# Latent attention with three-pass scores, joint keys of two heads, and the query factor inside the exponential

## The reference, cut to what matters

```python
def queries(cq, rotate):
    q = (_rms(cq) * q_norm) @ w_uq                              # 512 -> 16 heads x 96
    q = _rms(q.reshape(*q.shape[:2], MLA_HEADS, MLA_QK)) * q_gain
    return _rope_tail(q, cos, sin) if rotate else q             # rotates the last 32 of 96

def keys_values(ckv, k_rope, rotate):
    ukv = ((_rms(ckv) * kv_norm) @ w_ukv).reshape(..., MLA_HEADS, MLA_NOPE + MLA_V)
    k_nope, v = ukv[..., :MLA_NOPE], ukv[..., MLA_NOPE:]        # 64 and 64
    k_rope = jnp.broadcast_to(k_rope[:, :, None, :], ...)       # one rope part for all heads
    k = _rms(jnp.concatenate([k_nope, k_rope], axis=-1)) * k_gain
    return (_rope_tail(k, cos, sin) if rotate else k), v

s = jnp.einsum('bqhd,bkhd->bhqk', qi, k).astype(jnp.float32) * 96 ** -0.5
p = jax.nn.softmax(s, axis=-1)
out = jnp.einsum('bhqk,bkhd->bqhd', p, v)
```

## Time and profile before

| | us |
|---|---|
| median of three runs | 3789.0 |
| profiled execution, its own time | 3790.6 |
| its span, first to last instruction | 3787.6 |
| PE busy in the span | 3653.7 (96%) |
| DVE, ACT, POOL busy | 1750.0, 1493.2, 1263.2 |
| chain that ended last | PE 62%, DVE 5%, ACT 2%, issue 1% |
| mean granted TensorE clock | 0.987 of full speed |

### The profile page before, as it was taken

One profiled execution on the slowest core, in us unless ns is written; L12 is line 12 of the kernel. 1 busy time (PEld: TensorE's weight loads), 2 busy tenths in 40 slices (PEclk: granted clock), 3 DMA queues, 4 the chain that ended last, 5 costly groups with the idle time before them and its releaser, 6 DMA issues.

```text
span 3787.6 us, 53426 instructions
## 1 busy us (share of the span) xinstructions
PE 3653.7 (96%) x19878; PEld 2903.4 (77%) x19878; DVE 1750.0 (46%) x2574; ACT 1493.2 (39%) x2501; POOL 1263.2 (33%) x524
## 2 busy tenths in 40 slices
PE   7999999999989999999999999899989999999998
PEld 5875788888866667888777778688867777877886
DVE  4766652333456665443555552511156555252114
ACT  4343431222355553332555552422235555333222
POOL 3530422232320112444423334344433333434443
PEclk9999999999989999999999999999999999999999
DMA  5367212111210002322212213232222222222222
GB/s 210 115 226 293 82 63 67 61 62 64 75 61 17 23 23 73 100 97 97 95 62 68 68 68 100 69 104 94 95 78 73 68 68 68 89 84 84 99 94 89
DMA packets 84706, 333.79 MB, mean 88 GB/s; under 512 B 9520, under 2 KB 9648, under 8 KB 78000
## 3 DMA queue, kind: packets, MB, share of 16 engines
q1 hardware_dynamic: 83808, 329.22, 25.4%
q10 hardware_dynamic: 720, 2.10, 0.2%
HBM read 329.18 MB, written 2.10 MB: 87 GB/s over the span
## 4 chain that ended last, share of the span: by engine, by line
PE 62%; DVE 5%; ACT 2%; issue 1%; DVEq 0%; ACTq 0%
PE pB L2263 13%; PE pB L274 12%; PE pB L275 12%; PE pB L276 12%; PE pT L2321 1%; PE pT L1756 1%; DVE arena L901 1%; PE pO L2348 1%; PE pS L2293 1%; PE pB L1730 1%; PE pS L1747 1%; PE pO L274 1%; PE pO L276 1%; PE pO L275 1%; PE pO L2343 1%
## 5 line engine op out<-in xcount | busy, mean ns | idle before, releaser
L2828 POOL TENSOR_TENSOR w_lo<-w_raw,w_hi 128x1024 fp32r<-128x1024 f32 x520 | 1263.0, 2430 | 2502.3 <-ACT w_hi L320 2501.7
L274 PE MATMUL pB<-h_hi,w_hi 128*128 128x512 f32 x2102 | 832.2, 396 | 38.7 <-DVE h_lo L2756 15.5
L275 PE MATMUL pB<-h_lo,w_hi 128*128 128x512 f32 x2102 | 823.9, 392 | 0.0
L276 PE MATMUL pB<-h_hi,w_lo 128*128 128x512 f32 x2102 | 823.5, 392 | 0.0
L320 ACT ACTIVATE w_hi<-w_raw 128x1024 fp32r<-128x1024 f32 x520 | 547.6, 1053 | 479.7 <-PE pB L276 315.0
L274 PEld LDWEIGHTS pB<-h_hi,w_hi 128*128 128x128 f32 x2102 | 399.5, 190 | 134.1 <-issue 40.1
L276 PEld LDWEIGHTS pB<-h_hi,w_lo 128*128 128x128 f32 x2102 | 399.0, 190 | 83.8
L275 PEld LDWEIGHTS pB<-h_lo,w_hi 128*128 128x128 f32 x2102 | 399.9, 190 | 81.9 <-issue 1.2
L274 PE MATMUL pB<-b_hi,w_hi 128*128 128x512 f32 (+1 forms) x1080 | 399.6, 370 | 7.6 <-POOL w_lo L2828 6.5
L275 PE MATMUL pB<-b_lo,w_hi 128*128 128x512 f32 (+1 forms) x1080 | 394.7, 365 | 0.0
L276 PE MATMUL pB<-b_hi,w_lo 128*128 128x512 f32 (+1 forms) x1080 | 394.6, 365 | 0.0
(11 more groups left out here) (527 smaller groups left out, 5140.5 us busy)
## 6 DMA issues: line engine op xcount, KB each, us to landing
w_raw<-stream SPq DMA_DIRECT2D x520, 512.0 KB, 3.3
under<-ada SPq DMA_DIRECT2D x42, 1024.0 KB, 4.8
arena<-ada SPq DMA_DIRECT2D x6, 1024.0 KB, 17.2
x<-xT SPq DMA_DIRECT2D x1, 2048.0 KB, 8.2
out<-x SPq DMA_DIRECT2D x8, 256.0 KB, 2.1
...
```

Of the source, the lines that this page charges most:

```text
L274: pe.matmul(dst, lh, rh, start=(begin and k == 0), stop=False)
L275: pe.matmul(dst, lh, rl, start=False, stop=False)
L276: last = pe.matmul(dst, ll, rh, start=False, stop=(end and k == len(pairs) - 1))
L2828: pool.tensor_tensor(w_lo[:, s, :], w_raw[:, s, :], w_hi[:, s, :].bitcast(F32), ALU.subtract).then_inc(lo_ready, 1)
```

## The change

Four things change in the latent attention, and nothing outside it:
- Scores are three fp32r passes over split halves `mla_q` and `mla_k` (buffers by head parity, high in 0 and 1, low in 2 and 3) in place of one f32 product of `qf` and `kf`.
- K and C project the 64 plain key features of two heads at once, one on partitions 0 to 63, the other on 64 to 127; the odd head of a pair has its rope rows below its plain ones. The rope part of the key is multiplied by the factor on POOL (`pool_key_rope`).
- Squares of the rope rows are summed once ahead (turn SR), scaled and added on POOL to the squares of the keys (`pool_key_squares`), and one product with a matrix of two blocks of ones gives the sums of both heads.
- Query sums become eight products with one column, and the query factor, one number per query, is the `scale` of the exponential.

```diff
         def turns_beside(p):
-            a, b, g = 2 * p + 2, 2 * p + 3, p // 2
-            if p + 1 == PAIRS_A:
+            q, g = p + 1, p // 2
+            if q == PAIRS_A:
                 return [[] for _ in range(8)]
-            if p % 2:
-                return [[("K", a)], [("C", p + 1)], [("SQ", a), ("SK", a)], [("SC", p + 1), ("Q", b)], [("K", b)], [("SQ", b)],
-                        [("SK", b)], []]
-            return [[("K", a)], [("C", p + 1), ("K", b)], [("V", 3 * g), ("V", 3 * g + 1)], [("SQ", a), ("SK", a)],
-                    [("V", 3 * g + 2), ("SC", p + 1)], [("Q", b)], [("SQ", b), ("SK", b)], []]
+            values = [("V", 3 * g + i) for i in range(3)] if p % 2 == 0 else []
+            return [[("K", q)], [("C", q)] + values[0:1], [("Q", 2 * q + 1)], [("SK", q), ("SC", q)], values[1:2] + [("SQ", q)],
+                    values[2:3], [], []]
...
-        FIRST_TURNS = [("Q", 0), ("Q", 1), ("K", 0), ("K", 1), ("SQ", 0), ("SK", 0), ("C", 0), ("SC", 0), ("SQ", 1), ("SK", 1)]
+        FIRST_TURNS = [("Q", 0), ("Q", 1), ("SR", 1), ("SR", 0), ("SQ", 0), ("K", 0), ("C", 0), ("SK", 0), ("SC", 0)]
...
             elif what == "SQ":
-                pe.wait_ge(q_sq, n + 1)
-                pe.matmul(dst[0:QK_A, :], o96, hsq_q[n % 2][0:QK_A, :], start=True, stop=True).then_inc(q_sum, 1)
+                pe.wait_ge(q_sq, 2 * n + 2)
+                for e in range(2):
+                    rows_of = (const("upto")[:, QK_A - 1:QK_A], const("from")[:, ROPE:ROPE + 1])[e]
+                    for t in range(TB):
+                        last = pe.matmul(dst[:, e * TB + t:e * TB + t + 1], hsq_q[e][:, t * P:(t + 1) * P], rows_of, start=True, stop=True)
+                last.then_inc(q_sum, 1)
             elif what == "SK":
-                pe.wait_ge(k_sq, n + 1)
-                pe.matmul(dst[0:QK_A, :], o96, hsq_l[n % 2][0:QK_A, :], start=True, stop=True).then_inc(k_sum, 1)
+                pe.wait_ge(kr_step, 4)
+                pe.wait_ge(k_total, 2 * n + 1)
+                pe.matmul(dst, by_pair, hsq_k[1], start=True, stop=True).then_inc(k_sum, 1)
...
-            lhs = qf[0:QK_A, n % 4, t * P:(t + 1) * P]
-            pe.matmul(score[u % 2][:, 0:512], lhs, kf[0:QK_A, n % 4, 0:512], start=True, stop=True)
-            pe.matmul(score[u % 2][:, 512:TC], lhs, kf[0:QK_A, n % 4, 512:TC], start=True, stop=True).then_inc(a_s, 1)
+            pe.wait_ge(q_low, n + 1)
+            e = n % 2
+            r, o = ROWS_A[e], slice(t * P, (t + 1) * P)
+            q_hi, q_lo, k_hi, k_lo = mla_q[r, e, o], mla_q[r, 2 + e, o], mla_k[r, e, :], mla_k[r, 2 + e, :]
+            for a, b in ((0, 512), (512, TC)):
+                pe.matmul(score[u % 2][:, a:b], q_hi, k_hi[:, a:b], start=True, stop=False)
+                pe.matmul(score[u % 2][:, a:b], q_hi, k_lo[:, a:b], start=False, stop=False)
+                last = pe.matmul(score[u % 2][:, a:b], q_lo, k_hi[:, a:b], start=False, stop=True)
+            last.then_inc(a_s, 1)
...
-            act.activation(attP[:, u % 2, :], score[u % 2][:, 0:TC], ACT.Exp, bias=anm[:, u % 4:u % 4 + 1], scale=SCALE_A,
+            act.activation(attP[:, u % 2, :], score[u % 2][:, 0:TC], ACT.Exp, bias=anm[:, u % 4:u % 4 + 1], scale=q_col(u),
...
+        def act_key_high(act, n):
+            r = ROWS_A[n % 2]
+            act.wait_ge(k_scaled, n + 1)
+            act.wait_ge(k_roped, n + 1)
+            act.activation(mla_k[r, n % 2, :], k_wide[r, 2 + n % 2, :], ACT.Copy).then_inc(k_high, 1)
...
+        def dve_key_low(dve, n):
+            r, b = ROWS_A[n % 2], n % 2
+            dve.wait_ge(k_high, n + 1)
+            dve.tensor_tensor(mla_k[r, 2 + b, :], k_wide[r, 2 + b, :], mla_k[r, b, :].bitcast(F32), ALU.subtract).then_inc(head_ready, 1)
+
+        def pool_key_squares(pool, p):
+            for part in (1, 0):
+                pool.wait_ge(rope_sum_ready, 2 - part)
+                pool.wait_ge(k_sq, 2 * p + 2 - part)
+                pool.tensor_tensor(hsq_k[part], hsq_k[part], rope_sum[part], ALU.add).then_inc(k_total, 1)
+
+        def pool_key_rope(pool, n, behind):
+            b = n % 2
+            r, to = ((slice(0, ROPE), ROPE_A[0][0]), (slice(NOPE, P), slice(0, NOPE)))[b]
+            pool.wait_ge(*behind)
+            pool.wait_ge(kr_step, 7)
+            pool.wait_ge(k_ln, 3 * (n // 2) + 3)
+            if n >= 2:
+                pool.wait_ge(a_s, TB * (n - 1))
+            pool.tensor_tensor(k_wide[to, 2 + b, :], krope[r, :], k_rstd[r, :], ALU.mult).then_inc(k_roped, 1)
+            pool.wait_ge(k_roped, n + 1)
...
+            for p in range(PAIRS_A - 1):
+                g = G_HEADS + 3 * (p // 2)
+                pool_key_squares(pool, p + 1)
+                if p % 2 == 0:
+                    lo_parts(g + 4, g + 5)
+                pool_key_rope(pool, 2 * p + 2, (lo_ready, g + 5) if p % 2 == 0 else (k_total, 2 * p + 4))
+                if p % 2:
+                    lo_parts(g + 6, g + 7)
+                pool_key_rope(pool, 2 * p + 3, (lo_ready, g + 7) if p % 2 else (k_roped, 2 * p + 3))
+                if p % 2 == 0:
+                    lo_parts(g + 5, g + 6)
```

More of the change, by code:

```diff
@@ L1842, in act_turn @@
+                act.wait_ge(k_sum, 2 * n)
+                act.activation(hsq_k[1], src, ACT.Square).then_inc(k_sq, 1)
             elif what == "C":
-                act.wait_ge(c_raw, n + 1)
-                act.wait_ge(c_sum, n)
-                for e in range(2):
-                    last = act.activation(hsq_c[e][0:NOPE, :], src[0:NOPE, e * C:(e + 1) * C], ACT.Square)
-                last.then_inc(c_sq, 1)
+                act.wait_ge(k_raw, 2 * n + 2)
+                act.activation(hsq_k[0], src[:, 0:C], ACT.Square).then_inc(k_sq, 1)
+            elif what == "SR":
+                act.wait_ge(rope_summed, 2 - n)
+                act.activation(rope_sum[n], src if n else src[:, 0:C], ACT.Copy, scale=1.0 / NOPE).then_inc(rope_sum_ready, 1)
@@ L1848, in act_turn @@
             elif what == "SQ":
                 act.wait_ge(q_sum, n + 1)
[L1850 to L1851 removed]
+                act.activation(q_log, src[:, 0:2 * TB], ACT.Ln, bias=QK_A * EPS, scale=1.0).then_inc(q_ln, 1)
+                act.wait_ge(q_ln, 2 * n + 1)
+                act.activation(q_scale[:, n % 2 * 8:n % 2 * 8 + 8], q_log, ACT.Exp, scale=-0.5).then_inc(q_ln, 1)
             elif what == "SK":
[L1853 removed]
@@ L1865, in act_turn @@
+                act.wait_ge(k_scaled, 2 * n)
+                act.wait_ge(k_roped, 2 * n)
+                act.activation(k_rstd[:, C:TC], src, ACT.Ln, **w).then_inc(k_ln, 1)
+            elif what == "SC":
+                act.wait_ge(k_sum, 2 * n + 2)
+                act.activation(k_rstd[:, 0:C], src[:, 0:C], ACT.Ln, **w).then_inc(k_ln, 1)
+                act.wait_ge(k_ln, 3 * n + 2)
+                act.activation(k_rstd, k_rstd, ACT.Exp, scale=-0.5).then_inc(k_ln, 1)
             elif what == "V":
@@ L2087, in act_mla_in @@
             r = slice(NOPE, P)
-            places = [cq[:, j, :] for j in range(4)] + [ckv[:, j, C:TC] for j in range(2)] + [kraw[0][r, C:TC]]
-            places += [ckv[:, j, 0:C] for j in range(2)] + [kraw[0][r, 0:C]]
+            places = [cq[:, j, :] for j in range(4)] + [ckv[:, j, C:TC] for j in range(2)] + [krope[r, C:TC]]
+            places += [ckv[:, j, 0:C] for j in range(2)] + [krope[r, 0:C]]
             g0 = G_MLA[0]
@@ L2829, in lo_part, with lo_parts @@
                                    ).then_inc(lo_ready, 1)
-            with pool.Fori(0, G_ALL // SLOTS) as r:
+            def lo_parts(g0, g1):
+                for g in range(g0, g1):
+                    lo_part(g, g % SLOTS)
+            turns = G_HEADS // SLOTS
+            with pool.Fori(0, turns) as r:
+                for s in range(SLOTS):
+                    lo_part(r * SLOTS + s, s)
+            lo_parts(turns * SLOTS, G_HEADS + 3)
+            pool_key_squares(pool, 0)
+            pool_key_rope(pool, 0, (k_total, 2))
+            pool_key_rope(pool, 1, (k_roped, 1))
+            lo_parts(G_HEADS + 3, G_HEADS + 4)
+            for p in range(PAIRS_A - 1):
[9 more added lines that the diff above has]
+                    lo_parts(g + 5, g + 6)
+            turns = -(-(G_MLAOUT + 3) // SLOTS)
+            lo_parts(G_MLAOUT + 3, turns * SLOTS)
+            with pool.Fori(turns, G_ALL // SLOTS) as r:
                 for s in range(SLOTS):
@@ L3060, in weight_stream @@
             for e in range(2):
-                pair[:, e * 4:e * 4 + 4] = uq[:, (h + e) * QK_A + WITH_PARTNERS].reshape(4, P, P).transpose(1, 0, 2)
+                pair[:, e * 4:e * 4 + 4] = uq[:, (h + e) * QK_A + HEAD_ROWS[e]].reshape(4, P, P).transpose(1, 0, 2)
             queries.append(pair.reshape(P, KD * P))
-        keys_values = np.concatenate([ukv[:, h * P:(h + 1) * P].reshape(2, P, P).transpose(1, 0, 2) for h in range(h0, h0 + 4)], 1)
-        out += [queries[0], keys_values.reshape(P, KD * P), queries[1]]
+        heads = ukv[:, h0 * P:(h0 + 4) * P].reshape(2, P, 4, 2, NOPE)
```

(3 more changed lines are left out.)

275 lines of the change are left out of this document (151 added, 124 removed).

## The result

The changed kernel is slower: 3809.0 us (median of 5 runs, 3804.9 to 3809.9) against 3787.9, ratio 1.0049, interval 1.0039 to 1.0060. The forecast was 3762, range 3746 to 3778. The profiled execution has a span of 3806.0 us, against 3787.6 before.

What follows compares the result with a forecast made beforehand. A pair costs what PE issues plus gaps waiting for DVE or ACT. Savings of 3 x 2.7 (odd) + 4 x 4.24 (even) + 2.0 (last) = 27 us take the profiled 3790.6 to 3763.6, median 3762; range 3746 to 3778.

Steps and rivals of the forecast that it cites:

- PE's work: Latent attention: PE work falls 5.34 us a full pair, 39.4 us in all, from scores, key projections and square sums.
- at granted clock 1.00 (the 2.4 GHz level): Attention pairs: PE's clock read from the kernel before, where odd pairs take 38.97 us and even ones 42.43.
- Place 1: Odd pairs, slots 0 to 2: PE's transposes wait for DVE's copy behind rotary steps; plus 1.1, POOL's square sum plus 0.6.
- place 2: Odd pairs, slots 3 to 6: DVE's row of steps before the next pair's first scores leaves gaps of 3.1; plus 1.3.
- place 3: Even pairs: POOL's weight and key steps delay the next pair's first scores; gap 2.2 us, plus 1.1 (0 to 2.5).
- 0.6 to 1.8 long by their columns: Expected length in us of the new POOL operations, four a pair, 28 inside the loop.
- The price per collision: Loss when a DVE operation meets a POOL operation on the shared SBUF ports: 2.0 us each.
- The rival of one collision more a pair: One more DVE and POOL collision on the path in each of seven pairs: 14 us less gain, 3776; chance 0.11.
- I take no change: Start of the stage: first scores later, about 1120.5, but first transposes at 1126 to 1131 against 1127.59, so no change.
- Unit chain: Scores start to maximum 1.49 us, to exponential 1.18, to transposes 1.19; binds odd pairs' empty slot 7, plus 0.3.
- the slower rival: Every new POOL operation stops DVE on the path: 28 x 2.0 = 56 against 39.4, 17 us slower, 3806; chance 0.04.
- my three conditions for being wrong: PE's count per pair falls under 5 us, gaps sum over 6 us a pair, or the stage's start moves over 4.

Runs made afterwards that it cites:

- e9: e6 plus two moves: odd pairs' weight-chunk rounding on ACT from turn 4 to turn 6, last rotary step to behind turn 1's copy; 3768.8 us.
- e1: Changed kernel with unread f32 matmuls put into PE's long waits; 3789.6 us.
- e7: Kernel before the change, with turn 7's scores made to wait for DVE reductions that nobody needs; 3832.0 us.
- e6: e2 with the start reordered: ACT's rotary squares ahead of the context norm's factor, head 1's DVE work behind the first two maxima; 3776.6 us.
- e2: Changed kernel with all four new POOL steps of a pair (two square-sum additions, two rotary key products) moved to DVE; 3781.3 us.
- e3: Changed kernel with a constant as the exponential's scale and the maximum's factor, instead of a column of query factors; 3798.1 us.

## Why the prediction was wrong, point by point

- *PE's work:* right. Scores 1.05 (forecast 1.04), one-column sums 1.70 (1.8), one key projection and one key sum a pair. In e9, where the waits are short, PE is busy 33.17 us in the odd pair shown, 31.4 at full clock, and 35.89 in the even one; the forecast's PE work is 31.5 and 35.8. Five of e9's six pairs came within 0.5 us of the forecast.
- *The step that failed, the largest:* "at granted clock 1.00 (the 2.4 GHz level)" was read off and then taken over into every term and bound, so that the clock's cost stood at nothing. In the kernel before no wait in these pairs was longer than 0.8 us. I priced a longer wait at its length, though the earlier trace rows showed a cold record at 2.08 for 1.02 behind a wait of 3.10. Filling the waits took back 18 to 19 of the 44 us that the prediction missed (e1), and e7 shows the surcharge in the other kernel.
- *Places 1 to 3:* the waits were placed rightly and sized too small. PE stood 42.38 - 36.26 = 6.1 us in the odd pair, where the forecast leaves 4.8, and 4.0 in the even one, where it leaves 2.4. At full clock an odd pair would have taken at least 42.4 - 5.1 = 37.3 and an even one 39.5, 1.0 and 1.3 over the forecast; with the clock held (e1) they took 39.1 and 39.9, 2.8 and 1.7 over it, since PE's faster work covers less. Place 1 was forecast at 1.4 plus 0.6 and measured 2.20; place 2 at 3.1 over several waits, measured 0.87, 0.42 and 2.08. In place 3 I foresaw POOL's queue (2.2) and saw 2.12 ahead of the same scores.
- *POOL's operations:* "0.6 to 1.8 long by their columns" failed in part. The 32x768 product takes 2.2 us in the mean and the 128x512 addition 1.7 beside DVE (1.3 alone, at the start); the 128x256 addition takes 0.7. The price per collision, 2.0, was high for most: the rotary step, the key scale and the low half of the key became 0.8 to 1.2 us longer, a low half of a query 1.9. The rival of one collision more a pair, 14 us, was too small: the four POOL steps of a pair were worth 21.5 to 27.7 us in all, clock included. "DVE about 1 us higher a pair" was too low as well: from the first R to the last DVE was busy 175.7 us before and 188.7 after, 2 us a pair, with the collisions in it.
- *Start:* "I take no change" failed by 6.8 us to the first R, 8.9 to the first transposes; with pair 0's saving that did not come, 11.0 us. The first scores started at 1128.3, where I had 1120.5. The causes in the trace: DVE does both heads' rotary steps ahead of the context norm, while PE waits 5.36 us for ACT's squares behind it, then 3.66 for POOL's square sum and 7.28 ahead of the first scores. e6 got 10.6 us of the first maximum and 6.4 of the first R back against e2 by order alone.
- *Unit chain:* counted unchanged, in fact 0.15 us longer. e3 puts the direct cost at 0.1 to 0.5 us a pair. Of the last pair, which saved 0.7 and not 2.0, it explains 0.5 us (26.2 to 25.7 in e3); the other 0.8 stays open.
- *Rivals and chances:* the slower rival had the right sign and the right pair of engines, at 0.04, but its 3806, so near to the 3809, is luck. It asked 2.0 us for each of 28 POOL operations and had neither the clock nor the start; moving them off POOL gave 21.5 to 27.7 us (e2), 0.8 to 1.0 each with the clock in it. Of my three conditions for being wrong one held by far (the start, where the first scores came 11.3 us later), one by little (PE stood 6.0 to 6.2 us in the odd pairs), and PE's count did not fail.

Sum: 18.0 us in the odd pairs, 14.0 in three even ones, 11.0 in the start with pair 0, 1.3 in the last pair; that is the 44 us from 3763.6 to the 3807.8 that the profiled execution took.

Open: which of the short waits are followed by the slow clock. One of 0.87 us was, behind the one-column matmuls of L1725:
```profile
1282.66 1.84 PE L1725 MATMUL pB<-cm,under 128*128 128x1 f32 x16
1285.38 1.05 PE L1774 MATMUL pT<-cm,attP 128*128 128x128 f32 x4 [0.87 <-DVE xc L1977]
```
In windows of 1 us behind it:
```profile
1286.00:1287.00 1.00, 1.00 (x5) 0.98 (x5) 0.96 (x3) 0.62 (x1) 0.31 (x1) 0.50 0.00 0
```
In e9 the clock fell behind the same matmuls after only 0.33 us, while waits of 0.9 to 1.3 us elsewhere in e2 and e9 left it at 1.00. So the length of a wait alone does not tell whether the clock falls, and no run tested what else does.
